# Norms of a two-layer mixer block: the sum over features on token partitions, root and reciprocal on 128x4, and a product with the identity that spreads them

## What is computed

```python
def rmsnorm(x, g):
    xf = x.astype(jnp.float32)
    y = xf * lax.rsqrt(jnp.mean(xf * xf, axis=-1, keepdims=True) + EPS)
    return (y * g.astype(jnp.float32)).astype(x.dtype)

def modulate_in(x, g, shift, scale):
    return rmsnorm(x, g) * (1 + scale) + shift

# per layer
xl = xl + 0.5 * ml[2] * swiglu(modulate_in(xl, g[0], ml[0], ml[1]), f_in[0], f_out[0])
ol, oc = token_mixer(modulate_in(xl, g[1], ml[3], ml[4]), modulate_in(xc, ...), ...)
xl = xl + ml[5] * ol
xl = xl + 0.5 * ml[8] * swiglu(modulate_in(xl, g[2], ml[6], ml[7]), f_in[1], f_out[1])
# at the end
return rmsnorm(xl, g_final)
```

## Time and profile before

| | |
|---|---|
| median of 3 runs | 3038.77 us (3030.85, 3038.77, 3039.6) |
| the profiled execution | 3050.23 us, its span 3048.5 us |
| TensorE busy | 2874.7 us, 94% |
| VectorE busy | 1718.3 us, 56% |
| ScalarE busy | 856.6 us, 28% |
| GpSimd busy | 292.2 us, 10% |
| mean granted clock of TensorE | 0.959 |

### The profile page before, as it was taken

One profiled execution on the slowest core, in us unless ns is written; L12 is line 12 of the kernel. 1 busy time (PEld: TensorE's weight loads), 2 busy tenths in 40 slices (PEclk: granted clock), 3 DMA queues, 4 the chain that ended last, 5 costly groups with the idle time before them and its releaser, 6 DMA issues.

```text
span 3048.5 us, 39841 instructions
## 1 busy us (share of the span) xinstructions
PE 2874.7 (94%) x14770; PEld 2340.1 (77%) x14770; DVE 1718.3 (56%) x2840; ACT 856.6 (28%) x1147; POOL 292.2 (10%) x279
## 2 busy tenths in 40 slices
PE   6999999999779999999999899999998979999998
PEld 5888888877543578888888788888876744678887
DVE  7676676669673356766676772222247664443334
ACT  3221122141363332211221422112232264432222
POOL 1000000024322110000000100000004232000000
PEclk8999999999877999999999999999998979999999
DMA  5333333321220013333333232111212220123232
GB/s 201 117 117 124 111 117 139 103 77 55 56 59 7 21 49 117 117 122 107 123 118 117 76 110 70 62 55 63 74 50 84 74 66 7 55 81 101 91 99 84
DMA packets 63374, 264.94 MB, mean 87 GB/s; under 512 B 8880, under 2 KB 11824, under 8 KB 53680
## 3 DMA queue, kind: packets, MB, share of 16 engines
q1 hardware_dynamic: 50608, 180.17, 18.0%
q0 software_dynamic: 11520, 75.11, 7.6%
q10 hardware_dynamic: 1152, 8.39, 0.7%
HBM read 252.89 MB, written 2.10 MB: 84 GB/s over the span
## 4 chain that ended last, share of the span: by engine, by line
PE 83%; DVE 10%; ACT 4%; issue 2%; DMA 1%; POOL 0%; ACTq 0%; SPq 0%; DVEq 0%
PE ps L1431 74%; PE ps L1670 2%; DVE conv_acc L1184 2%; PE ps L1597 2%; PE ps L1625 1%; PE ps L1605 1%; DVE w_lo L934 1%; DVE rstd L987 1%; DVE nmax L1289 1%; ACT e_sb L846 1%; DMA x<-in_xT 1%; ACT probs_t L860 1%; DVE mod_start_acc L1366 1%; DVE y_hi L1023 0%; DVE sq L1011 0%
## 5 line engine op out<-in xcount | busy, mean ns | idle before, releaser
L1431 PE MATMUL ps<-y_hi,w_hi 128*128 128x512 f32 (+1 forms) x3184 | 912.5, 350 | 65.3 <-DVE y_lo L1015 31.2
L1431 PE MATMUL ps<-y_lo,w_hi 128*128 128x512 f32 (+1 forms) x3184 | 907.8, 349 | 0.0
L1431 PE MATMUL ps<-y_hi,w_lo 128*128 128x512 f32 (+1 forms) x3184 | 900.6, 346 | 0.0
L1431 PEld LDWEIGHTS ps<-y_hi,w_hi 128*128 128x128 f32 x3184 | 519.9, 191 | 164.5 <-issue 35.8
L626 ACT ACTIVATE w_hi<-w_raw 128x1024 fp32r<-128x1024 f32 (+1 forms) x290 | 326.6, 1128 | 1063.9 <-PE ps L1431 1063.9
L1431 PEld LDWEIGHTS ps<-y_lo,w_hi 128*128 128x128 f32 x3184 | 517.1, 190 | 75.9
L1431 PEld LDWEIGHTS ps<-y_hi,w_lo 128*128 128x128 f32 x3184 | 515.0, 190 | 77.7 <-issue 0.2
L934 DVE TENSOR_TENSOR w_lo<-w_raw,w_hi 128x1024 fp32r<-128x1024 f32 (+1 forms) x290 | 384.8, 1327 | 322.3 <-ACT w_hi L626 320.0
L949 DVE SCALAR_TENSOR_TENSOR mod_acc<-mod_raw,cact,mod_acc 128x256 f32<-128x256 f32 x896 | 360.2, 479 | 0.0
L1431 PE MATMUL ps<-h_lo,w_hi 128*128 128x512 f32 (+1 forms) x1254 | 356.8, 344 | 0.0
L1431 PE MATMUL ps<-h_hi,w_hi 128*128 128x512 f32 (+1 forms) x1254 | 356.3, 344 | 0.0
(11 more groups left out here) (162 smaller groups left out, 2033.8 us busy)
## 6 DMA issues: line engine op xcount, KB each, us to landing
w_raw<-in_w_up SPq DMA_DIRECT2D x176, 512.0 KB, 3.5
mod_raw<-in_w_mod POOLq DMA_DIRECT2D x64, 1024.0 KB, 5.1
w_raw<-in_w_down SPq DMA_DIRECT2D x64, 704.0 KB, 4.1
w_raw<-in_w_in SPq DMA_DIRECT2D x36, 512.0 KB, 3.5
mod_start<-in_w_mod ACTq DMA_DIRECT2D x8, 1024.0 KB, 22.0
w_raw<-in_w_out SPq DMA_DIRECT2D x16, 512.0 KB, 3.5
stack<-qk_hi SPq DMA_DIRECT2D x48, 96.0 KB, 2.1
band<-in_rpb POOLq DMA_DIRECT2D x16, 224.0 KB, 6.6
```

Of the source, the lines that this page charges most:

```text
L1431: mm = pe.matmul(slot[s][:, at:at + b - a], w[s][:, k, :], r[:, k, a:b], start=(k == 0 and n == 0), stop=(k == kc - 1 and n == 2))
```

## The change

The sum over features is now asked for with the squares as the stationary operand and one column of ones as the moving one: 128 tokens at a time come out on 128 partitions, one column for each block of 128 tokens. Root and reciprocal then work on 128 x 4 (512 tokens) or 128 x 2 (256 tokens), in two new small tiles. A new step on TensorE, `widen_root`, multiplies the reciprocals, each column repeated 128 times as the stationary operand, by the identity, which puts the reciprocal of every token on all partitions, in the same PSUM tile `turn`. VectorE's multiplication of the first half and the final scaling read it from there. For the second half ScalarE copies it to `rstd` (`keep_root`), since GpSimd reads it from SBUF. `invert_root(1)` moves from m == 6 to m == 5 in VectorE's list.

```diff
@@ root, keep_root (ScalarE)
-                act.activation(rstd[:, a:b], turn[:, LAT * half:LAT * half + b - a], ACT.Sqrt, bias=eps_t[:, 0:1], scale=1.0 / D).then_inc(sems["norm_sqrt"], 1)
+                act.activation(std_t[:, a // P:b // P], turn[:, LAT * half:LAT * half + (b - a) // P], ACT.Sqrt, bias=eps_t[:, 0:1],
+                               scale=1.0 / D).then_inc(sems["norm_sqrt"], 1)
+
+            def keep_root(tokens):
+
+                a, b, _ = halves(tokens)[1]
+                norms[0] += 1
+                act.wait_ge(sems["rstd_wide"], 2 * norms[0])
+                act.activation(rstd[:, a:b], turn[:, LAT:LAT + b - a], ACT.Copy).then_inc(sems["rstd"], 1)
@@ start of the list of ScalarE, ahead of make_y(0, 0, TOK)
+            keep_root(TOK)
@@ down_last, after (ScalarE)
                     if m == 4:
                         root(p.tokens, 1)
+                    if m == 6:
+                        keep_root(p.tokens)
@@ invert_root (VectorE)
-                dve.reciprocal(rstd[:, a:b], rstd[:, a:b]).then_inc(sems["rstd"], 1)
-                t.wait("rstd")
+                dve.reciprocal(rstd_t[:, a // P:b // P], std_t[:, a // P:b // P]).then_inc(sems["norm_inverse"], 1)
@@ make_y (VectorE)
+                t.wait("rstd_wide")
+                t.skip("rstd_wide")
-                        dve.tensor_tensor(sq[m % 2][:, a0:b0], x[:, m, a0:b0], rstd[:, a0:b0], ALU.mult).then_inc(sems["normed0"], 1)
+                        dve.tensor_tensor(sq[m % 2][:, a0:b0], x[:, m, a0:b0], turn[:, 0:b0 - a0], ALU.mult).then_inc(sems["normed0"], 1)
@@ down_last, after (VectorE)
-                    if m == 6:
+                    if m == 5:
                         invert_root(p.tokens, 1)
@@ final scaling (VectorE)
+                t.wait("rstd_wide")
                 for m in range(DC):
-                    dve.scalar_tensor_tensor(o_final[:, m, a:b], x[:, m, a:b], gain_f[:, m:m + 1], rstd[:, a:b],
+                    dve.scalar_tensor_tensor(o_final[:, m, a:b], x[:, m, a:b], gain_f[:, m:m + 1], turn[:, LAT * half:LAT * half + b - a],
@@ norm_reduce, widen_root (TensorE)
-                for src, last in ((ssq, False), (sq[1], True)):
-                    pe.wait_ge(sems["square" if last else "sum_squares"], (squares_made if last else ssq_made)[0])
-                    mm = pe.matmul(turn[:, LAT * half:LAT * half + b - a], ones[:, :], src[:, a:b], start=not last, stop=last)
+                pe.wait_ge(sems["sum_squares"], ssq_made[0])
+                pe.wait_ge(sems["square"], squares_made[0])
+                for j in range((b - a) // P):
+                    for src, last in ((ssq, False), (sq[1], True)):
+                        mm = pe.matmul(turn[:, LAT * half + j:LAT * half + j + 1], src[:, a + P * j:a + P * j + P], ones[:, 0:1],
+                                       start=not last, stop=last)
                 mm.then_inc(sems["norm_sum"], 1)
+
+            def widen_root(tokens, half):
+
+                a, b, _ = halves(tokens)[half]
+                t.wait("norm_inverse")
+                for j in range((b - a) // P):
+                    c = a // P + j
+                    mm = pe.matmul(turn[:, LAT * half + P * j:LAT * half + P * j + P], rstd_t[:, c:c + 1].to_broadcast([P, P]),
+                                   ident[:, :], start=True, stop=True)
+                mm.then_inc(sems["rstd_wide"], 1)
@@ run_last (TensorE)
+                        if s == 0 and k == p.kc // 3 + 4:
+                            widen_root(p.tokens, 0)
@@ body (TensorE)
+                                if half == 0 and step == 6 and pair0:
+                                    widen_root(p.tokens, 1)
@@ start and end of TensorE's list
             t.wait("inputs", 16 * 11)
+            widen_root(TOK, 0)
+            widen_root(TOK, 1)
...
             norm_reduce(LAT, 1)
+            widen_root(LAT, 1)
```

More of the change, by code:

```diff
@@ L184 @@
     "mod_raw", "mod_sum", "mod_vec", "cond_silu", "mod_step",
-    "hidden_hi", "hidden_lo", "square", "sum_squares", "norm_sum", "norm_sqrt", "rstd",
+    "hidden_hi", "hidden_lo", "square", "sum_squares", "norm_sum", "norm_sqrt", "norm_inverse", "rstd_wide", "rstd",
     "early_done", "updated", "normed0", "normed1", "affine", "y_hi", "y_lo", "scale_ready", "gates_ready",
@@ L262, in trunk @@
     lam = place("lam", [P, 8])
+    std_t = place("std_t", [P, TOK // P])
+    rstd_t = place("rstd_t", [P, TOK // P])
     nmax = place("nmax", [P, 4])
@@ L584, in normalize @@
                 norms[0] += 1
-                pool.wait_ge(sems["rstd"], 2 * norms[0])
+                pool.wait_ge(sems["rstd"], norms[0])
                 for m in range(DC):
@@ L663, in _ @@
             hidden = [0]
+            norms = [0]
             for b in range(MOD_FIRST):
```

## The result

| | kernel before | changed kernel |
|---|---|---|
| first measurement, median | 3037.66 us (4 runs, 3030.85 to 3039.60) | 3066.19 us (4 runs, 3065.00 to 3067.74) |
| ratio | | 1.0091, interval 1.0072 to 1.0110 |
| measured again later (h1_after) | 3047.93 us (27 runs, 3036.45 to 3061.57) | 3062.83 us (10 runs, 3060.06 to 3066.67) |
| ratio | | 1.0046, interval 1.0028 to 1.0063 |
| profiled execution | 3050.23 us | 3067.74 us |

The forecast was 3041 us, 2.7 us above the kernel before, and "the same" with a chance of 0.75. The change makes the kernel slower, by 28.5 us as first measured and by 14.9 us when measured again. The changed kernel's median fell by 3.4 us.

A forecast was written before the change was run, and what follows sets the result against it. TensorE's big products were taken as the bound (74% of what ends last), the reciprocal 1%. Terms +1.8 +0.2 +0.2 -1.2 +1.4 +0.3 +0 gave +2.7 on 3038.8, put at 3041 us; own range 3033 to 3045.

The forecast's parts named there:

- Start, +1.8: Kernel start: TensorE's small passes at the slow pace throughout bring `mod_vec` at 58.05 instead of 56.23, +1.8 us.
- First halves: gain and spreading cancel: Second norm's pattern: the shorter reciprocal gains at most 0.96 us, and the spreading on TensorE costs 0.96 us.
- Norm 3, -1.2: Norm after the first `mix_out`: 0.9 us gained in the first half and 0.3 in the second, -1.2 us.
- norm 6, +0.3: Norm after the second `mix_out`: first reciprocal already covered, spreading costs 0.48 us, second half returns part, +0.3 us.
- Last norm, 0: Last norm: first half's spreading costs 0.48 us, the end gains 0.6; -0.1 us, taken as 0.
- Second halves, 0 in norms 2 and 4, +1.4 in norm 5: Second halves: gain used up by `keep_root` waiting for the spreading; ahead of the second `mix_in`, lower clock adds 1.4 us.
- step 5: Six products in TensorE's list ahead of the second half's spreading, starting at 636.52 and priced at 1.45 us.
- the chain at 639.0: Second norm, second half: products, spreading, drain and copy end at 639.0, against 638.89 where chunk 7's scaling started before.
- the spreading falls on the lower clock: Rival, chance 0.13: at 1.2 GHz step 5 takes 2.6 us, spreading 0.92; +8.6 us, 3047 us.
- the dearer operand: Rival, chance 0.04: a repeated-column operand or one-column pass costs twice the nearest row; +4.8 on top, 3045.5 us.
- The base: Whole kernel: the 3038.8 us median of the kernel before, to which the forecast added 2.7 us.
- The width of 22 us: Whole kernel: the forecast's whole range, from 3028 us up to the two slower cases.

The follow-up runs named there:

- h1_after: The changed kernel itself, tiles where they stand, measured again beside the kernel before: 3062.83 us, ratio 1.0046.
- f1: Kernel before with 32 unused bytes per partition ahead of `nmax`, the measure for f2, f3 and f4: 3041.67 us.
- f2: The whole change with its two tiles behind `rstd` and 32 unused bytes ahead of `nmax`, other tiles as in f1: 3050.86 us.
- f3: f2 with the second half of the five norms between phases done as before (wide sum, no `keep_root`, no second spreading): 3041.83 us.
- f4: f2 with 128 columns of ones instead of one as the moving operand of the sum: 3039.13 us.
- e1_pad64: Kernel before with an unused tile of 64 bytes per partition ahead of `nmax`, so tiles lie as in the changed kernel: 3046.76 us, ratio 1.0013.
- e2: Changed kernel with its two new tiles in unused room behind `rstd`, every other tile at its address in the kernel before: 3062.01 us, ratio 1.0041.
- h3: f4 with the second half's spreading at step 5 of TensorE's list instead of step 6: 3029.47 us, ratio 0.9943.
- i4: h3, the same file, measured again with more rounds: 3032.10 us, ratio 0.9945.

## Why the prediction was wrong

The steps, against f1 and f2 where the addresses are equal:

- **Start, +1.8.** +1.0 (56.58 to 57.57), +1.3 between the two first profiles. Right in kind: the slow pace throughout, 13.79 us for the 64 passes (forecast 13.8) and 2.91 for the spreading (2.8). Rows below. The granted clock can't be read there: the view gives 1.00 from the first product to about 85 us, but the passes are 0.22 us apart, as in the kernel before from 36 to 45 us, where it gives 0.50. The Trainium skill ("TensorE: Matmul & The Clock Gate", LDWEIGHTS) gives a weight load as its columns / 1.2 ns, with no second length for the other clock. The trace does not agree: a pass, which has one load, takes 0.11 us at one clock and 0.22 at the other.
- **First halves: gain and spreading cancel.** Right where the clock stayed up. f3 has the new first half and the old second half: norm 2 32.62 against 32.61, norm 4 32.60 against 32.60. The first multiplication comes 1.6 us earlier there (5.25 instead of 6.87 us after the last sum of squares), but ScalarE's first scaling does not (7.62 against 7.65), since its split waits for unit 0, as forecast. In the changed kernel's second norm the 16 passes are eight rows 0.22 apart, 1.8 us (1.73 forecast), and the eight passes of spreading take 0.97 (0.96 forecast), from 631.58 to the next product at 632.55.
- **Norm 3, -1.2; norm 6, +0.3.** f3 has -1.05 and +0.42. Right.
- **Last norm, 0.** +0.30: the spreading cost 0.67 instead of 0.48, and the end gained 0.35 instead of 0.6, since the four passes ran at the lower clock (1.22 us for L1474 at 3056.43).
- **Second halves, 0 in norms 2 and 4, +1.4 in norm 5.** This step failed. It took step 5 at 1.45 us, the time at full clock, and put the chain at 639.0. At full clock the chain is right: in f4, where the second norm kept 2.4 GHz, the spreading stands behind step 5, `keep_root` waits 1.54 us, and the norm takes 32.61 us as without the change. In f2 the clock fell in every one of the five norms. The only ground for the full clock was that the trace of before shows that pace there; but it had it with sums of 256 and 512 columns, and the change took just these columns out. The rival with its place, mechanism and price stood in the text ("the spreading falls on the lower clock"): 1.6 us for a norm, +8.6 in sum. Measured is 1.4 to 1.6 for the second half of norms 2, 4 and 5 (19.80 to 20.01 us instead of 18.37 from the first multiplication to the eighth `y_lo`), 1.9 for norm 3 (33.49 against f3's 31.56), and +9.2 in sum. What the rival lacked is the first half: where the clock fell there too (norms 2 and 5 of f2, norm 2 of the changed kernel), the first multiplication comes 6.8 us after the last sum of squares instead of 5.25, another 1.6 us. So the mechanism was seen and its chance, 0.13, was the error. (Two slips in the sums change nothing here: this rival's 3047 us lies under the 3047.9 from which "slower" counts, though its chance was put there; and the dearer operand's terms give 3046.3, not 3045.5.)
- **The base.** The sum was set on a median of three runs, 3038.8. Later runs of the same kernel have 3047.8 with a range of 40 us. The width of 22 us was thus too narrow even for a kernel that does not change.

TensorE's timeline at the start of the changed kernel (answers the earlier trace rows):

```profile
34.20 13.79 PE L1730 MATMUL ps<-cact,mod_start 128*128 128x2 f32 x64
47.86 2.91 PE L1474 MATMUL ps<-ident,rstd_t 128*128 128x128 f32 x12
50.56 6.83 PE L1740 MATMUL ps<-ones_r,mod_start_acc 128*128 128x1 f32 x32
```

Of the 28.5 us first measured, then, about 10 are the norms' and the start's own steps (9.2 by the medians on equal addresses, 11.3 by their table, 10.4 between the first profiles). This part is shown. Some 10 are the first median of the kernel before (3037.7 against 3047.8 later) and 3.4 that of the changed kernel. The remaining 4 to 6 lie in the phases. In the two first profiles these take 7.1 us more, of which the first mixer has only 0.7, since it ran slow in both; the rest is the pace that goes with the addresses of e1_pad64. The medians add to that how often the first mixer keeps the higher clock, and whether the change has a part in this is open.

## What to carry to other kernels

Where a change replaces wide products by narrow ones on an engine that also waits there, price the products behind it at both clocks, and ask what is queued behind them; a short step that others wait for belongs ahead of such a queue, not behind it. A small product may be worth widening: 128 equal columns cost 0.11 us for a pass, as one does, and f4 came out 11.7 us under f2, 2.9 of them at the start. And before a change of 1% is read, run the kernel before with some bytes of unused room: here 32 bytes moved the median by 5 to 6 us, against 9.2 for the whole change, and they also made the measurement quiet.

## What the runs showed of the hardware

- The pace of back-to-back products with weights loaded between them depends on where the tiles lie: for 512 and 256 columns together 346.7, 350.8, 352 or 353.4 ns, for 512 alone in the last phases 226.7 ns (before, e2), 228.9 (64 bytes), 232.4 (128) and 233.3 (32). The placement that is fastest in the first phases is slowest in the last. The placement of the kernel before changes its pace from phase to phase, in another order in e2_tail than in the kernel before; those with 32 and 128 bytes more keep one pace in all phases with 768 tokens.
- A pass of the sum took 0.11 us at 2.4 GHz and 0.21 to 0.22 at 1.2 GHz, with one column (f2) and with 128 (f4) alike: rows of two passes start 0.22 and 0.43 us apart in both. The forecast had 0.12 for 128.
- One step of the first mixer's attention took 2.8 us where the granted clock was 1.00 and 5.3 where it was 0.50 (e1_pad64 from 935.26 to 938.02, h1_after from 941.18 to 946.47, starts of two row maxima that follow each other), and the same kernel shows both in different executions (2.76 us in h3, 5.29 in i4).
